# State-space layer: its parameters made in layer 0's second feed-forward part, gelu taken between the parts of the last scan, and another order of its products

## The reference, cut to what matters

```
h = x @ ab_w_in
u = h[:, :512]                         # 32 groups of 16
lb = exp(lam * dt)                     # complex, one per group and state
f  = (lb - 1) / lam
state[t] = lb * state[t-1] + f * (b @ u[t])
y  = gelu(real(c @ state) + d * u)
out_a = y * sigmoid(y @ w_glu)
out_b = (window_mean(h[:, 512:]) - h[:, 512:]) @ pool_w * pool_scale
mix = concat(out_a, out_b) @ ab_w_out
```

## Time and profile before

| what | value |
|---|---|
| three runs | 1832.81, 1834.44, 1835.70 us |
| profiled execution, its own time | 1834.42 us |
| its span | 1832.7 us |
| mean granted TensorE clock | 0.983 of full speed |
| TensorE busy (matmul) | 1754.3 us, 96% |
| VectorE busy | 916.4 us, 50% |
| ScalarE busy | 624.0 us, 34% |
| 16 DMA engines, both data queues | 59.4% of the span |

### The profile page before, as it was taken

One profiled execution on the slowest core, in us unless ns is written; L12 is line 12 of the kernel. 1 busy time (PEld: TensorE's weight loads), 2 busy tenths in 40 slices (PEclk: granted clock), 3 DMA queues, 4 the chain that ended last, 5 costly groups with the idle time before them and its releaser, 6 DMA issues. The chain is left out here.

```text
span 1832.7 us, 24660 instructions
## 1 busy us (share of the span) xinstructions
PE 1754.3 (96%) x10010; PEld 1325.4 (72%) x10010; DVE 916.4 (50%) x1318; ACT 624.0 (34%) x834; POOL 112.1 (6%) x91
## 2 busy tenths in 40 slices
PE   6999999999999999998999989999998999999996
PEld 5888878788878888786778877755554878755553
DVE  3655757554566447676865767211114577311113
ACT  3543443454334434434544543100002453111000
POOL 1000060000000000511000000000001000000000
PEclk9999999999999999999999988999998999999998
DMA  7455541655365545325444414999995523999992
GB/s 271 182 195 191 188 158 35 219 186 190 151 230 186 187 177 207 115 92 201 161 171 181 161 54 177 386 420 422 422 423 212 203 93 138 374 421 421 423 421 119
DMA packets 59618, 419.78 MB, mean 229 GB/s; under 512 B 6704, under 2 KB 6704, under 8 KB 10256
## 3 DMA queue, kind: packets, MB, share of 16 engines
q1 hardware_dynamic: 55728, 404.78, 57.2%
q0 software_dynamic: 3808, 13.83, 2.2%
HBM read 417.53 MB, written 1.05 MB: 228 GB/s over the span
## 5 line engine op out<-in xcount | busy, mean ns | idle before, releaser
L1763 DVE TENSOR_TENSOR w_lo<-raw,w_hi 128x2048 fp32r<-128x2048 f32 x181 | 411.1, 2289 | 148.5 <-ACT w_hi L1340 147.8
L1340 ACT ACTIVATE w_hi<-raw 128x2048 fp32r<-128x2048 f32 x193 | 365.0, 1913 | 60.0 <-DMA raw<-units 59.9
L589 PE MATMUL hh<-w_hi,xt_hi 128*128 128x512 f32 x704 | 279.8, 397 | 1.8 <-DVE xt_lo L1870 1.8
L591 PE MATMUL hh<-w_hi,xt_lo 128*128 128x512 f32 x704 | 275.3, 391 | 0.0
L590 PE MATMUL hh<-w_lo,xt_hi 128*128 128x512 f32 x704 | 275.1, 391 | 0.0
L589 PE MATMUL y<-w_hi,xt_hi 128*128 128x512 f32 (+1 forms) x464 | 186.1, 401 | 4.3 <-DVE xt_lo L1870 2.7
L590 PE MATMUL y<-w_lo,xt_hi 128*128 128x512 f32 (+1 forms) x464 | 181.2, 391 | 0.0
L591 PE MATMUL y<-w_hi,xt_lo 128*128 128x512 f32 (+1 forms) x464 | 181.2, 390 | 0.0
L589 PEld LDWEIGHTS hh<-w_hi,xt_hi 128*128 128x128 f32 x704 | 132.8, 189 | 30.0 <-DVE xt_lo L1870 2.9
L591 PEld LDWEIGHTS hh<-w_hi,xt_lo 128*128 128x128 f32 x704 | 132.7, 188 | 28.4
L589 PE MATMUL y<-w_hi,ht_hi 128*128 128x512 f32 x368 | 146.0, 397 | 6.6 <-DVE w_lo L1763 6.4
(11 more groups left out here) (327 smaller groups left out, 2140.4 us busy)
## 6 DMA issues: line engine op xcount, KB each, us to landing
raw<-units SPq DMA_DIRECT2D x289, 1024.0 KB, 10.4
late<-units SPq DMA_DIRECT2D x96, 1024.0 KB, 11.3
ln_gb<-ln_g POOLq DMA_DIRECT2D x6, 512.0 KB, 4.0
ln_gb<-ln_b POOLq DMA_DIRECT2D x6, 512.0 KB, 5.2
x_rows<-x POOLq DMA_DIRECT2D x2, 512.0 KB, 9.9
ln_gb<-ln_mix_g POOLq DMA_DIRECT2D x2, 512.0 KB, 4.0
ln_gb<-ln_mix_b POOLq DMA_DIRECT2D x2, 512.0 KB, 5.1
ln_gb<-ln_ffn_g POOLq DMA_DIRECT2D x2, 512.0 KB, 4.3
```

The lines of the kernel that those rows point to most:

```text
L589: pe.matmul(dst, left[0], right[0], start=start, stop=False)
L591: return pe.matmul(dst, left[1], right[0], start=False, stop=stop)
L1340: act.activation(hi[r][:, :], raw[r][:, :], ACT.Copy).then_inc(hi_ready, 1)
L1763: dve.tensor_tensor(lo[r][:, :], raw[r][:, :], hi[r][:, :].bitcast(F32), ALU.subtract)\
```

## The change

Four things are done.

1. VectorE's `s5_parameters` is cut in two, `s5_parameters` and `s5_powers`; both become asides of steps 1 and 2 of layer 0's second feed-forward part, ScalarE's `s5_parameters` one of step 1 there. In layer 1 the angles and sines move up to step 1, one weight matrix is made per step, and `s5_weights` runs one step later (c = j - 6 and c = j - 7).
2. Half of the small copies of quarter 0 go to VectorE, which takes them from `u_p`, ahead of its split of unit 7. Semaphores `u_copied` and `u_shared` tie them.
3. `s5` and `g1` get two separate places each. TensorE's order becomes: features 3, states 2, window means, outputs 0, states 3, pool mix, outputs 1, outputs 2, three pool parts, outputs 3, gate.
4. VectorE does scans 0, 1 and 2 in a row, then gelu part 0 of quarter 0, then scan 3 with the pool's low part and gelu parts of quarters 0 and 1 between its steps, then the other parts, interleaved. The splits of units 8 and 9 move behind. ScalarE's gelu steps are interleaved in the same manner; it loads the sigmoid table ahead of its split of unit 9.

```diff
@@ s5_weights, on TensorE and on ScalarE
-                c = j - 5 if at > 0 else j - 6
+                c = j - 6 if at > 0 else j - 7
@@ states(c), TensorE
+                    if c == 0:
+                        pe.wait_ge(u_shared, 1)
@@ TensorE's order
                 features(3)
+                states(2)
                 window_means()
-                states(2)
                 outputs(0)
+                states(3)
                 pool_mix()
-                states(3)
                 outputs(1)
+                outputs(2)
                 pe.wait_ge(xt_lo_ready, seen(xt_lo_ready))
                 pool_part(0, 0)
-                outputs(2)
                 pool_part(0, 1)
+                pool_part(1, 0).then_inc(unit_used, 1)
                 outputs(3)
-                pool_part(1, 0).then_inc(unit_used, 1)
@@ features(m), ScalarE
-                    act.activation(u_p[:, m], src, ACT.Copy)
-                    for q in range(4):
+                    act.activation(u_p[:, m], src, ACT.Copy).then_inc(u_copied, 1)
+                    for q in range(2 if m == 0 else 4):
@@ s5_and_pool, ScalarE
+                act.preload_act_table(ACT.Sigmoid)
                 split_to(S5_UNITS)
...
+                square(0)
+                sigmoid(0)
+                high(0)
+                square(1)
+                sigmoid(1)
+                square(2)
+                high(1)
+                sigmoid(2)
+                high(2)
+                square(3)
+                sigmoid(3)
+                high(3)
@@ asides, ScalarE
                 if l < DEPTH - 1:
-                    gated()
+                    gated(aside=(s5_parameters,))
                 else:
-                    gated(aside=(s5_parameters, s5_sines, s5_outputs), beside=s5_weights)
+                    gated(aside=(s5_sines, s5_outputs), beside=s5_weights)
@@ asides, VectorE
-                return (s5_parameters, lambda: (s5_angles(), out_weights(1)), lambda: (out_weights(2), out_weights(3)),
+                return (s5_angles, lambda: out_weights(1), lambda: out_weights(2), lambda: out_weights(3),
                         lambda: (out_weights(4), in_weights(0))) + tuple(lambda c=c: in_weights(c) for c in range(1, 4))
...
-                    gated(3 * l + 2)
+                    gated(3 * l + 2, aside=(s5_parameters, s5_powers))
@@ s5_and_pool, VectorE
+                split_to(6)
+                dve.wait_ge(dve_link, seen(dve_link, 2))
+                dve.wait_ge(u_copied, 1)
+                for q in range(2, 4):
+                    for k in range(CHUNK):
+                        ins = dve.tensor_copy(u_s[32 * k:32 * k + 32, 0, q, :], u_p[32 * q:32 * q + 32, 0, CHUNK - 1 - k, :])
+                ins.then_inc(u_shared, 1)
                 split_to(7)
...
-                    if c == 0:
-                        dve.wait_ge(bu_ready, 2)
-                    elif c >= 2:
+                    meanwhile(3)
+                    if c >= 2:
                         dve.wait_ge(y_part, c - 1)
...
                 scan(0)
+                scan(1)
+                scan(2)
+                gelu(0, 0)
+                scan(3, ((pool_low,), (part(0, 1),), (part(1, 0), part(0, 2)), (part(0, 3), part(1, 1))))
+                for c, n_ in ((2, 0), (1, 2), (2, 1), (1, 3), (2, 2)):
+                    gelu(c, n_)
                 split_to(8)
+                for c, n_ in ((3, 0), (2, 3), (3, 1), (3, 2), (3, 3)):
+                    gelu(c, n_)
                 split_to(S5_UNITS)
```

More of the change, by code:

```diff
@@ L398, in program @@
         m5 = carve(work, 0, 2, 2, 4 * N_CHUNKS)
-        s5 = carve(work, 1024, 2, 2, 4, N_CHUNKS)
+        s5 = [carve(v, at, 2, 4, N_CHUNKS) for v, at in ((params, 0), (work, 1024))]
         y5 = carve(work, 2048, 4, T)
@@ L404, in program @@
         ab_row = [pool_rows[:, t, :] for t in range(TT)]
-        g1 = pool_rows[:, 0, 0:T]
+        g1 = [pool_rows[:, 0, b * T:(b + 1) * T] for b in range(2)]
         lam_in = carve(params, 0, DEPTH, 4, HD)
@@ L1625, in s5_and_pool, with square, sigmoid, high @@
                 ins.then_inc(xt_hi_ready, 1)
+                act.preload_act_table(ACT.Sigmoid)
                 split_to(S5_UNITS)
-                for c in range(4):
+                def square(c):
                     act.wait_ge(y_read, c + 1)
-                    act.activation(g1, y5[:, c], ACT.Square).then_inc(s5_act, 1)
+                    act.activation(g1[c % 2], y5[:, c], ACT.Square).then_inc(s5_act, 1)
+                def sigmoid(c):
                     act.wait_ge(s5_dve, seen(s5_dve))
-                    act.activation(g1, g1, ACT.Sigmoid, scale=GELU_C * 0.044715).then_inc(s5_act, 1)
+                    act.activation(g1[c % 2], g1[c % 2], ACT.Sigmoid, scale=GELU_C * 0.044715).then_inc(s5_act, 1)
+                def high(c):
                     act.wait_ge(s5_dve, seen(s5_dve))
                     act.activation(xt_hi[:, c, :], y5[:, c], ACT.Copy).then_inc(xt_hi_ready, 1)
+                square(0)
[10 more added lines that the diff above has]
+                high(3)
                 split_to(S5_UNITS + 1)
@@ L2213, in gelu @@
                         dve.wait_ge(s5_act, seen(s5_act))
[L2214 to L2215 removed]
+                        dve.scalar_tensor_tensor(out=g1[c % 2], in0=g1[c % 2], scalar=1.0 / 0.044715, in1=y5[:, c],
+                                                 op0=ALU.add, op1=ALU.mult).then_inc(s5_dve, 1)
                     elif part == 2:
                         dve.wait_ge(s5_act, seen(s5_act))
[L2218 removed]
+                        dve.tensor_tensor(y5[:, c], y5[:, c], g1[c % 2], ALU.mult).then_inc(s5_dve, 1)
                     else:
@@ L2222, in gelu, with scan, meanwhile @@
                             .then_inc(xt_lo_ready, 1)
-                def scan(c):
+                def scan(c, between=((), (), (), ())):
+                    def meanwhile(n_):
+                        for piece in between[n_]:
+                            piece()
                     def wide(v):
@@ L2255, in scan, with pool_low, part @@
                     dve.wait_ge(st_ready, c + 1)
-                scan(0)
-                split_to(8)
-                scan(1)
-                dve.wait_ge(xt_hi_ready, seen(xt_hi_ready))
-                for g in range(4):
-                    ins = dve.scalar_tensor_tensor(out=xt_lo[:, 4 + g, :],
-                                                   in0=y_bank[g // 2][1][:, (g % 2) * T:(g % 2 + 1) * T],
-                                                   scalar=pool_scale[:, g:g + 1], in1=xt_hi[:, 4 + g, :].bitcast(F32),
-                                                   op0=ALU.mult, op1=ALU.subtract)
-                ins.then_inc(xt_lo_ready, 1)
-                scan(2)
-                for part in range(4):
-                    gelu(0, part)
-                scan(3)
+                def pool_low():
+                    dve.wait_ge(xt_hi_ready, seen(xt_hi_ready))
+                    for g in range(4):
+                        ins = dve.scalar_tensor_tensor(out=xt_lo[:, 4 + g, :],
+                                                       in0=y_bank[g // 2][1][:, (g % 2) * T:(g % 2 + 1) * T],
+                                                       scalar=pool_scale[:, g:g + 1], in1=xt_hi[:, 4 + g, :].bitcast(F32),
+                                                       op0=ALU.mult, op1=ALU.subtract)
+                    ins.then_inc(xt_lo_ready, 1)
+                def part(c, n_):
+                    return lambda: gelu(c, n_)
+                scan(0)
+                scan(1)
[4 more added lines that the diff above has]
+                    gelu(c, n_)
+                split_to(8)
+                for c, n_ in ((3, 0), (2, 3), (3, 1), (3, 2), (3, 3)):
+                    gelu(c, n_)
                 split_to(S5_UNITS)
-                for c in range(1, 4):
-                    for part in range(4):
-                        gelu(c, part)
                 split_to(S5_UNITS + 1)
```

13 lines of the change are left out of this document (9 added, 4 removed).

## The result

The changed kernel takes 1821.47 us (median of four runs, 1819.41 to 1822.26); the kernel before took 1834.56 us beside it (four runs). The ratio is 0.9929, with a 95% interval from 0.9917 to 0.9942: 13.1 us less. Forecast were 1826.2 us, 8.2 less. So the direction was right and the forecast gain 5 us too small: the time lies within the range given for 8 in 10 (1820 to 1831) and outside the forecast's own (1823 to 1829). The profiled execution took 1822.09 us, 12.3 less than that of before; the stages are compared on it.

A forecast was written before the change was run, and what follows sets the result against it. TensorE, busy 96% of the span, was taken as the bound, losing time only in waits and half clock. Terms 12.8 + 1.1 - 1.3 - 4.4 = 8.2 us gave 1826.2 us; own range 1823 to 1829, 8 in 10 1820 to 1831.

The forecast's parts named there:

- the layer: State-space layer: new order and shared copies gain 12.8 us, 7 to 15 by the bounds.
- The waits of VectorE in scan 3: State-space layer: the new order adds two VectorE waits for ScalarE, 0.6 and 1.2 us.
- the gate's end: State-space layer: the gate ends at 1087.0 and not 1104.1, 17.1 us earlier.
- Behind the gate: TensorE's wait for the product with the gate's sigmoid grows from 1.37 to 3.7 us, plus 2 us of half clock.
- layer 0: Layer 0's second feed-forward part: TensorE newly waits 1.3 us, no half clock; 3.4 us by the skill page's table-load drain.
- the beginning of layer 1's part: Layer 1's second feed-forward part: unit 8 is ready 1.1 us earlier, not 5.7; the lower clock stays.
- its end: Layer 1's second feed-forward part, before step 10: 2.4 us of wait and 2.0 of half clock, 4.4 us lost.
- One weight matrix fewer in a step moves nothing that TensorE waits for.: Layer 1's second feed-forward part: making fewer weight matrices in a step changes no TensorE wait, so no gain was counted.
- A: Rival, chance 0.2: more gained, no half clock at step 10 or behind the gate, or splits find a gap; 1822 us.
- B: Rival, chance 0.13: gain mostly given back, by copies of 0.42 us each (1831.7) or half clock in layer 0 (1828 to 1832).
- C: Rival, chance 0.05: slower, TensorE's small products in the state-space layer leave it at 1.2 GHz; 1835, up to 1845 us.
- D: Rival, chance 0.07: the parameter wait moves whole to layer 0 (5.7 us plus 2 of half clock); 1832.6 us.

The follow-up runs named there:

- e1: The kernel before with only the parameter moves, layer 1's asides and `s5_weights` as changed; median 2.3 us below the kernel before.
- e4: The changed kernel, but ScalarE makes all 16 small copies of quarter 0; the state-space layer is 1.8 us longer.
- e7: The changed kernel, but VectorE runs scan 3 whole, with the pool's low part and gelu parts behind it; the layer is 4.6 us longer.
- e10: The changed kernel with TensorE's old order of products in the state-space layer; the layer takes 80.58 us, 2.4 less than with the new order.
- e6: The changed kernel, but layer 0's parameters stand after steps 2 and 3, not 1 and 2; layer 0's stage fell by 1.35 us.
- e8: The changed kernel, but VectorE's split of unit 10 stands behind the product with the gate's sigmoid and its low parts; 3.2 us less in the layer.
- e5: The changed kernel, but ScalarE's sines stand after step 2 of layer 1's second feed-forward part, not step 1; that stage fell by 8.0 us.
- e11: The changed kernel, but VectorE again makes two weight matrices after step 3 of layer 1's second feed-forward part; stage 210.60 us against 207.5.
- e2: The changed kernel without the parameter moves and new weight asides, only the state-space layer's edits; no slower than the whole change.
- e12: The changed kernel with outputs 3 ahead of the third pool part on TensorE; the layer gained 0.3 us.

## Why the prediction was right, and by what it was short

**Right: the layer.** Forecast 12.8 us, measured 13.9. VectorE's eight small copies are the form of which no row was there; they took 1.59 us, 0.20 each as assumed. Timeline of VectorE after, at the layer's start:

```profile
1047.40 1.59 DVE L2230 COPY work<-work 32x64 f32<-32x64 f32 x8 [0.15 <-ACT work L1610]
```

The waits of VectorE in scan 3 (forecast 0.6 and 1.2, measured 0.75 and 1.20), outputs 3 without a wait, and the gate's end (17.1 and 17.2 us earlier) came as worked out. Behind the gate TensorE waits 3.1 us and not 3.7; the half clock there lasts 2.56 us at 0.50 and costs 1.3, where I took 2. Those two terms were 1.3 us too dear, about the 1.1 by which the layer was under-sized.

No step of the prediction had the norm behind the layer. There seven matmuls ran at half clock in the kernel before, at 1120 us, and none after: 1.6 of the 2.1 us of that stage. The stretch between the norm's two marks, before and after:

```profile
1115.57:1125.79 10.22, 8.38 (x42) 6.65 (x40) 7.08 (x12) 4.28 (x4) 1.59 (x1) 0.83 0.37 110
```

```profile
1105.18:1113.78 8.60, 6.76 (x42) 5.50 (x40) 7.08 (x11) 4.29 (x4) 1.59 (x1) 1.00 0.40 133
```

The instructions are the same, yet it is hardly chance: the two traces with the layer's old code (before and e1) have 10.2 us there, and the twelve with the new code 8.4 to 8.6. So the 1.6 us seem to go with the layer's edits; what decides them is not shown, and two traces of the old code are few.

How the layer's 13.9 us divide is shown in part. By the marks, taking back the shared copies costs 1.8 us (e4), the pieces within scan 3 cost 4.6 (e7), and TensorE's new order is a loss of 2.4 (e10). The rest of the change of the layer (three scans in a row, two places for `s5` and `g1`, the later split of unit 8, gelu of quarters 1 to 3 interleaved, the early table load) was made together, and no run takes it apart.

The table load was the place where page and row stood apart. Timeline of ScalarE after, in the layer:

```profile
1071.13 1.28 ACT L1630 ACT_TABLE_LOAD   x1
1072.42 1.91 ACT L1344 ACTIVATE w_hi<-raw 128x2048 fp32r<-128x2048 f32 x1
```

The next activation starts 0.01 us after the load. The wait in layer 0 is 1.50 us, near the 1.3 that go with the row, and not the 3.4 that would go with a drain as the Trainium skill has it ("ScalarE: Activation LUTs", What ACT_TABLE_LOAD costs). No row of this case shows a drain.

**Right: layer 0.** 1.84 us by the marks for 1.3 forecast, with no half clock behind the wait.

**Right: the beginning of layer 1's part.** Unit 8's wait is 4.51 us (forecast 4.6), since the sines stand ahead of its copy. Timeline of ScalarE after:

```profile
860.92 1.06 ACT L1567 ACTIVATE work<-work 128x1024 f32<-128x1024 f32 x1 [5.48 <-DVE work L2169]
...
864.16 3.69 ACT L1344 ACTIVATE w_hi<-raw 128x2048 fp32r<-128x2048 f32 x2
```

The step took 1.9 us less, 1.15 from the wait and the rest from fewer matmuls of 0.6 us or more (7 and not 11). That rest is luck: e4, e6, e7, e8 and e10, with the same code and the same wait, had 11 or 12. e5 shows that this order is the cause: without it the whole wait goes.

**Right: its end.** 2.12 us of wait (forecast 2.4) and 1.3 to 1.7 us of half clock (forecast 2.0). From the end of step 4 to the stage's mark the changed kernel loses 3.9 us, where 4.4 were forecast. ScalarE's split stands ahead of the copy as supposed. ScalarE after, before step 10:

```profile
1001.80 0.59 ACT L1372 ACTIVATE ht_hi<-turn 128x512 fp32r<-128x512 f32 x1
1002.28 1.91 ACT L1344 ACTIVATE w_hi<-raw 128x2048 fp32r<-128x2048 f32 x1
1004.08 0.60 ACT L1596 ACTIVATE work<-turn 128x512 f32<-128x512 f32 x1
```

**Wrong: "One weight matrix fewer in a step moves nothing that TensorE waits for."** TensorE waited 1.95 us at the turned gate of step 4, because VectorE made two matrices after step 3 and took a split before it came to the product. With one matrix per step that wait is gone (the row at 909.24 above has none) and the step takes 16.82 us, not 18.96: 2.1 us. The view of waits held it as `turn L705`, five waits, longest 1.9; it was passed over because the three larger entries were enough for a story. e11 brings it back by this edit alone.

**The account.** In the stages touched, 8.2 us were forecast. The layer gave 1.1 more, the begin of layer 1's part 0.8 more, its end 0.5 less lost, layer 0 0.5 more lost; step 4's wait 2.1, not forecast. That makes 12.2. The stage behind the layer gave another 2.1, and the untouched stages took 1.7 back, both mostly by clock: 12.5 us, the difference of the spans. So the mechanisms named carry the forecast 8.2; of what came on top, step 4's wait is a gain that the prediction denied, the norm's clock one that it did not have, and some 0.8 us behind unit 8 are luck.

**The rivals.** A (more is gained: 1822, at most 1819.5) is where the time came out, but by none of its mechanisms: half clock followed both waits, and the splits found no gap. B, C and D did not happen: copies of 0.20 us, full clock in the small products, and 1.5 us in layer 0 in place of 5.7. Of the change's parts, TensorE's new order brought nothing beside the new order of VectorE (e10), which I had taken as part of the gain.

## What to carry to other kernels

Read the whole list of the bound engine's waits against the diff, the small entries too: an edit that takes work out of one step can remove a wait that no argument names. Work moved ahead of a copy on an in-order engine delays everything behind it: three sines ahead of one split cost about 6 us of the stage, a split ahead of the product with the gate's sigmoid 1.7 us of wait, and both went by changing the place alone. Where two engines' orders are changed together, put each back by itself: here one of them was a loss under the other.

## What was not expected of the hardware

Half clock behind a short wait is not a property of the wait. Behind 1.9 to 2.1 us ahead of the first states it came in full (before, 0.56 over 7.8 us), by half (e1, 0.78) or not at all (e4, 1.00). Behind 2.1 us at step 10 it came in nine traces of ten (0.72 to 0.76 over 6.2 us), and not in e5 (1.00); behind 1.9 to 2.0 us at step 4, in none of three (before, e2, e11: 1.00). Behind waits of 2.6 us and more at the places of this account it came in every trace: eight times behind the 3.1 us after the gate, ten times behind 4.5 us and twice behind 5.7 us on unit 8. Behind 1.5 us in layer 0 and 1.4 us after the gate it came in none, ten traces and five. The Trainium skill ("TensorE: Matmul & The Clock Gate", HAM oscillation) describes such a loss: waits for data after which the next products run at the lower clock. Here waits of about two microseconds were followed by it in some executions and not in others.

This sets what the medians can tell. The eleven runs of e1, one program, reach from 1829.05 us (mean clock 0.989) to 1836.59 us (0.984), and their time goes largely with the granted clock. Of the 40 runs of the kernel before that stand beside the experiments, four took 1828.8 to 1829.5 us at 0.988, the other 36 took 1832.9 to 1837.6 at 0.983 or 0.984. An effect of 1 to 3 us, such as e11's or e12's, is read between the marks of a trace and not in a median.
